# Pooling stage: tokens loaded first, band table converted on GpSimd, smaller scaling blocks, new engine orders

## What is computed

```python
def rmsnorm(x, g):
    xf = x.astype(jnp.float32)
    return xf * lax.rsqrt(jnp.mean(xf * xf, axis=-1, keepdims=True) + EPS) * g

def pool_mixer(h, w, scale):             # L = 272 tokens, D = 1024
    for g, win in enumerate((2, 4, 8, 16)):
        xg = hf[..., g * 256:(g + 1) * 256]
        cs = jnp.cumsum(xg, axis=1)
        lag = jnp.pad(cs[:, :-win], ((0, 0), (win, 0), (0, 0)))
        cnt = jnp.minimum(pos + 1, win)[None, :, None]
        outs.append((cs - lag) / cnt - xg)
    pooled = jnp.stack(outs, axis=2)
    return jnp.einsum('blgc,gcd->blgd', pooled, w).reshape(B, L, D) * scale

h = h + pool_mixer(rmsnorm(h, norm_mix), pool_w, pool_scale)
h = h + swiglu(rmsnorm(h, norm_ffn), w_gate, w_up, w_down)
```

## Time and profile before

| | |
|---|---|
| three runs | 1027.3, 1028.75, 1030.66 us |
| the profiled execution | 1028.95 us, of which the span of the engines' work is 1027.1 us and 1.85 us lie around it |
| TensorE busy | 992.3 us |
| mean granted TensorE clock over the span | 0.986 of full speed |

### The profile page before, as it was taken

How to read it: one execution, slowest core, us unless ns; L and a number is a source line. 1 busy time by engine, 2 the same in 40 slices (tenths; PEclk the granted TensorE clock), 3 DMA queues, 4 the chain that set the end, 5 groups by cost and what they waited for, 6 DMA issues and landing times.

```text
span 1027.1 us, 19786 instructions
## 1 busy us (share of the span) xinstructions
PE 992.3 (97%) x7900; PEld 963.3 (94%) x7900; DVE 816.1 (79%) x1350; ACT 521.2 (51%) x839; POOL 174.6 (17%) x178
## 2 busy tenths in 40 slices
PE   8999999999999899999999999789999999999997
PEld 6999999999988799999999998668999999999996
DVE  4887889985999889989898679999776787676542
ACT  5644443344666546464535347575445565545332
POOL 4400000220333351400056100000001330000011
PEclk7999999999999999999999999999999999999998
DMA  8467667894333348877687324342334565555541
GB/s 321 168 210 221 218 204 240 272 333 164 124 123 123 104 125 322 276 265 245 209 273 249 125 65 157 113 144 84 123 103 146 177 212 177 192 169 189 158 143 41
DMA packets 53685, 187.69 MB, mean 183 GB/s; under 512 B 6104, under 2 KB 7801, under 8 KB 53146
## 3 DMA queue, kind: packets, MB, share of 16 engines
q1 hardware_dynamic: 53594, 186.42, 54.8%
HBM read 185.35 MB, written 1.05 MB: 181 GB/s over the span
## 4 chain that ended last, share of the span: by engine, by line
PE 85%; DVE 10%; issue 2%; ACT 1%; DMA 1%; POOL 0%; SPq 0%; DVEq 0%; POOLq 0%; ACTq 0%
PE psum L429 84%; DVE memr L962 3%; DVE memr L976 2%; PE psum L444 1%; DVE memr L1015 1%; DVE mem L1148 1%; DMA mem<-in_pool_first 1%; ACT memr L1599 1%; DVE psum L1358 1%; DVE mem L1366 0%; DVE mem L1340 0%; ACT mem L1859 0%; DVE mem L1342 0%; DVE mem L1364 0%; DVE mem L1010 0%
## 5 line engine op out<-in xcount | busy, mean ns | idle before, releaser
L429 PE MATMUL psum<-memr 128*128 128x256 f32 (+5 forms) x7640 | 954.9, 288 | 24.2 <-DVE memr L976 11.7
L429 PEld LDWEIGHTS psum<-memr 128*128 128x128 f32 (+2 forms) x7640 | 932.9, 190 | 44.1 <-issue 24.4
L962 DVE TENSOR_TENSOR memr<-mem,memr 128x1024 fp32r<-128x1024 f32 (+1 forms) x290 | 357.4, 1269 | 49.8 <-ACT memr L1596 49.8
L1596 ACT ACTIVATE memr<-mem 128x1024 fp32r<-128x1024 f32 (+2 forms) x296 | 290.4, 1027 | 28.0 <-DMA mem<-in_w_down 10.4
L1599 ACT ACTIVATE memr<-mem 128x256 fp32r<-128x256 f32 (+4 forms) x168 | 80.3, 489 | 275.8 <-DVE mem L1078 113.7
L976 DVE TENSOR_TENSOR memr<-mem,memr 128x256 fp32r<-128x256 f32 (+2 forms) x129 | 63.8, 502 | 12.8 <-ACT memr L1599 12.1
L1599 ACT ACTIVATE memr<-psum 128x256 fp32r<-128x256 f32 (+4 forms) x112 | 44.8, 438 | 41.7 <-PE psum L444 23.2
L1063 DVE TENSOR_TENSOR mem<-psum,mem 128x256 f32<-128x256 f32 (+1 forms) x66 | 28.0, 424 | 47.6 <-PE psum L429 47.6
L972 DVE CUSTOM_DVE_ANT_0 mem<-mem 128x1024 f32<-128x1024 f32 x48 | 62.6, 1304 | 0.6
L2070 POOL TENSOR_TENSOR mem<-mem 128x256 f32<-128x256 f32 (+1 forms) x6 | 4.0, 671 | 314.5 <-DVE mem L1094 150.7
L976 DVE TENSOR_TENSOR memr<-psum,memr 128x256 fp32r<-128x256 f32 (+4 forms) x96 | 45.8, 496 | 12.8 <-ACT memr L1599 11.5
(11 more groups left out here) (138 smaller groups left out, 458.9 us busy)
## 6 DMA issues: line engine op xcount, KB each, us to landing
mem<-in_w_gate SPq DMA_DIRECT2D x66, 512.0 KB, 4.4
mem<-in_w_up SPq DMA_DIRECT2D x66, 512.0 KB, 4.5
mem<-in_w_ada SPq DMA_DIRECT2D x48, 512.0 KB, 4.6
mem<-in_w_down SPq DMA_DIRECT2D x48, 448.0 KB, 4.3
mem<-in_w_in SPq DMA_DIRECT2D x40, 512.0 KB, 3.7
mem<-in_w_down SPq DMA_DIRECT2D x24, 512.0 KB, 4.5
mem<-in_sb_qkv SPq DMA_DIRECT2D x24, 512.0 KB, 4.6
mem<-in_sb_o SPq DMA_DIRECT2D x8, 512.0 KB, 4.3
```

What stands on the lines that cost most here:

```text
L429: return pe.matmul(out, a, b, start=start, stop=stop)
L962: dve.tensor_tensor(r(ol, n), raw(e), rf(oh, n), ALU.subtract).then_inc(w_lo, 1)
L1596: act.activation(r(oh, n), raw(e), ACT.Copy).then_inc(w_hi, 1)
```

## The change

1. **Loads.** The token blocks are loaded in the order 0, 2, 1. The first-token table and a new small table (its low part, now computed on the host) follow, then the band table, as a tensor of its own. The constants move behind six weight tiles, epsilon becomes a memset, and `SILC` moves behind three more weight tiles, for which SyncE waits on GpSimd.
2. **Conversions.** VectorE no longer converts the two tables; GpSimd does, in two copies, before its weight tiles. Its subtraction for the low part goes. The host makes the high part exactly representable.
3. **Scaling.** The tokens are scaled in blocks of 256, 256 and 512 columns instead of 512 and 512.
4. **Waits.** The reciprocal no longer stands behind the wait for the tables, and the root no longer waits for the constants. TensorE waits for the tokens per `pooled(i)`, and for the constants in `mean_square`.
5. **Orders.** TensorE: `pool_mix(0)` and `(1)` come before `pooled(4)` and `pooled(6)`; 7 warm-up products instead of 8. VectorE and ScalarE follow. On ScalarE, weight tile 4 stands behind `pool_norm(0)` and tile 5 behind `pool_norm(1)`. The one Silu over `SILC` moves from m = 0 to m = 2 of the first SwiGLU.

```diff
-    WARM, NWARM = st.take(512), 8
+    WARM, NWARM = st.take(512), 7
+    XCOLS = ((0, 256), (256, 256), (512, 512))
...
 (TensorE)
         def pooled(i):
             g = i // 2
+            pe.wait_ge(x_lo, (3, 6, 9, 9)[g])
...
-        pe.wait_ge(pre_dve, 6)
-        pe.wait_ge(pre_pool, 2)
-        pe.wait_ge(x_lo, 3)
+        pe.wait_ge(pre_pool, 3)
         for i in range(4):
             pooled(i)
-        pe.wait_ge(x_lo, 6)
+        pool_mix(0)
         pooled(4)
         pooled(5)
-        pool_mix(0)
+        pool_mix(1)
         pooled(6)
         pooled(7)
-        pool_mix(1)
         pool_mix(2)
         pool_mix(3)
...
 (VectorE)
-        dve.wait_ge(band_in, 32)
-        dve.tensor_copy(r(BH, 4 * 144), f(BAND, 4 * 144)).then_inc(pre_dve, 1)
         dve.wait_ge(pre_act, 2)
         dve.reciprocal(f(SS + 6, 3), f(SS + 3, 3)).then_inc(pre_dve, 1)
-        dve.tensor_copy(r(BH + 4 * 144, 4 * T0, 0, 16), f(BAND + 4 * 144, 4 * T0, 0, 16)).then_inc(pre_dve, 1)
...
+        scaled_low(0)
+        scaled_low(1)
+        pooled_low(0)
+        pooled_low(1)
+        scaled_low(2)
+        pooled_low(2)
+        pooled_low(3)
         pool_add(0)
+        pooled_low(4)
+        pooled_low(5)
+        pool_norm(0)
+        pool_add(1)
         pooled_low(6)
         pooled_low(7)
-        pool_add(1)
-        pool_norm(0)
+        pool_norm(1)
         pool_add(2)
-        pool_norm(1)
+        pool_norm(2)
         pool_add(3)
-        pool_norm(2)
         pool_norm(3)
         low_halves(W_FFN[0] + 6)
...
 (ScalarE)
-        act.wait_ge(cst_in, 16)
         act.activation(f(SS + 3, 3), f(SS, 3), ACT.Sqrt, bias=epsc).then_inc(pre_act, 1)
...
+        scaled_high(0)
+        high_halves(1)
+        scaled_high(1)
         act.wait_ge(vec_in, 16)
-        for i in range(4):
-            pooled_high(i)
-        high_halves(6)
+        pooled_high(0)
+        pooled_high(1)
+        high_halves(2)
+        scaled_high(2)
+        pooled_high(2)
+        pooled_high(3)
+        high_halves(4)
         pooled_high(4)
         pooled_high(5)
         pool_norm(0)
+        high_halves(5)
         pooled_high(6)
         pooled_high(7)
-        for g in range(1, 4):
-            pool_norm(g)
+        pool_norm(1)
+        high_halves(6)
+        pool_norm(2)
+        pool_norm(3)
         high_halves(W_FFN[0] + 6)
...
 (GpSimd)
-        pool.wait_ge(pre_dve, 6)
-        pool.tensor_tensor(firsts(r, BL, 16), firsts(f, BAND + 4 * 144, T0), firsts(rf, BH + 4 * 144, T0),
-                           ALU.subtract).then_inc(pre_pool, 1)
+        pool.wait_ge(first_in, 32)
+        pool.tensor_copy(r(BH + NBAND, NALL - NBAND, 0, 16), f(BAND + NBAND, NALL - NBAND, 0, 16)).then_inc(pre_pool, 1)
+        pool.wait_ge(band_in, 16)
+        pool.tensor_copy(r(BH, NBAND), f(BAND, NBAND)).then_inc(pre_pool, 1)
...
 (SyncE)
-        for i, (lo, n) in enumerate(ROWS):
+        for i in (0, 2, 1):
+            lo, n = ROWS[i]
             sp.dma_start(f(HTOK + D * i, D, 0, n), T["htok"][lo:lo + n]).then_inc(htok_in[i], 16)
-        sp.dma_start(f(CST, C_POOL), T["cst"][:, 0:C_POOL]).then_inc(cst_in, 16)
-        sp.dma_start(f(BAND, 4 * 144), T["cst"][:, C_POOL:]).then_inc(band_in, 16)
-        sp.dma_start(f(BAND + 4 * 144, 4 * T0, 0, 16), T["pool_first"]).then_inc(band_in, 16)
+        sp.dma_start(f(BAND + NBAND, 4 * T0, 0, 16), T["pool_first"]).then_inc(first_in, 16)
+        sp.dma_start(f(BAND + NBAND + 4 * T0, 4 * 16, 0, 16), T["pool_rest"]).then_inc(first_in, 16)
+        sp.dma_start(f(BAND, NBAND), T["band"]).then_inc(band_in, 16)
+        raws(1)
         sp.dma_start(f(VEC, NVEC), T["vecs"]).then_inc(vec_in, 16)
-        raws(NRAW)
+        raws(4)
         sp.dma_start(f(H, KT * T0), T["ht"]).then_inc(h_in, 16)
+        raws(6)
+        sp.dma_start(f(CST, NCONST), T["cst"]).then_inc(cst_in, 16)
+        raws(9)
         sp.dma_start(f(SILC, 2048), T["c2"].partition_broadcast(128)).then_inc(c_in, 16)
```

More of the change, by code:

```diff
@@ L29 @@
     NVEC += _c
-C_ID, C_ONE, C_EPS, C_TRI, C_POOL = 0, 128, 256, 257, 433
-NCONST = C_POOL + 4 * 144
+C_ID, C_ONE, C_TRI, NCONST = 0, 128, 256, 432
+NBAND = 4 * 144
 ROWS = ((16, 128), (0, 16), (144, 128))
@@ L44, in constants @@
     c[:, C_ONE:C_ONE + 128] = 1.0 / D
-    c[:, C_EPS] = EPS
     q, k = np.arange(128)[:, None], np.arange(176)[None, :]
     c[:, C_TRI:C_TRI + 176] = np.where(k < q, 0.0, NEG)
-    first = np.zeros((16, 4 * T0), np.float32)
+    band, first = np.zeros((128, NBAND), np.float32), np.zeros((16, 4 * T0), np.float32)
     for g, w in enumerate(WINDOWS):
         s, t = np.arange(128)[:, None], np.arange(144)[None, :]
-        c[:, C_POOL + 144 * g:C_POOL + 144 * (g + 1)] = ((t >= s) & (t < s + w)) / w - (t == s)
+        band[:, 144 * g:144 * (g + 1)] = ((t >= s) & (t < s + w)) / w - (t == s)
         s, t = np.arange(16)[:, None], np.arange(T0)[None, :]
@@ L54, in constants @@
         first[:, T0 * g:T0 * (g + 1)] = np.where((t >= s) & (t < s + w), np.float32(1) / count, np.float32(0)) - (t == s)
-    return c, first
+    high = (first.view(np.uint32) & np.uint32(0xFFFFF000)).view(np.float32)
+    rest = np.concatenate([(first - high)[:, T0 * g:T0 * g + 16] for g in range(4)], axis=1)
+    return c, band, high, rest
 def tables():
@@ L213, in build @@
     AH, AL = top.take(KT * T0), top.take(KT * T0)
-    CST = top.take(C_POOL)
+    CST, EPSC = top.take(NCONST), top.take(1)
     VEC = top.take(NVEC)
@@ L234, in build @@
     XH, XL = st.take(3 * D), st.take(3 * D)
-    NBAND = 4 * 144 + 4 * T0
-    BAND, BH, BL = st.take(NBAND), st.take(NBAND), st.take(4 * 16)
+    NALL = NBAND + 4 * T0 + 4 * 16
+    BAND, BH = st.take(NALL), st.take(NALL)
+    BL = BH + NBAND + 4 * T0
+    XCOLS = ((0, 256), (256, 256), (512, 512))
     SS = st.take(11)
-    WARM, NWARM = st.take(512), 8
+    WARM, NWARM = st.take(512), 7
     sil = Area(WORDS - 3 * 1024, WORDS)
@@ L305, in build @@
     OUTS = ((0, 2), (2, 2), (4, 2), (6, 1), (7, 1))
-    ident, ones, epsc = f(CST + C_ID, 128), f(CST + C_ONE, 128), f(CST + C_EPS, 1)
+    ident, ones, epsc = f(CST + C_ID, 128), f(CST + C_ONE, 128), f(EPSC, 1)
     def vec(name, i=0, p1=128):
@@ L319, in a_lo @@
         return r(AL + i * T0 + n0, n)
-    def firsts(m, o, w):
-        return m(o, 4 * w, 0, 16).rearrange("p (g w) -> p g w", g=4)[:, :, 0:16]
     def pb(b, n=512, p0=0, p1=128, at=0):
@@ L457, in mean_square @@
             b = bank(("ms", root), root_done, root)
+            pe.wait_ge(cst_in, 16)
             pe.wait_ge(sq_done, 7 * (s + 1))
@@ L469, in x @@
                 return r(half + D * src + 128 * i, 128, 0, n)
-            fb = r(BH + 4 * 144 + T0 * g, T0, 0, 16)
+            fb = r(BH + NBAND + T0 * g, T0, 0, 16)
             mm(pb(b, T0), x(XH, 1, 16), fb, True, False)
@@ L976, in minus @@
             return dve.tensor_tensor(out, x, hi, ALU.subtract)
+        dve.memset(f(EPSC, 1), EPS)
         dve.memset(f(SS, 11), 1.0).then_inc(pre_dve, 1)
@@ L986, in vector, with scaled_low @@
                                      op0=ALU.mult, op1=ALU.add, accum_out=f(SS + i, 1, 0, n)).then_inc(pre_dve, 1)
-        dve.wait_ge(band_in, 32)
-        dve.tensor_copy(r(BH, 4 * 144), f(BAND, 4 * 144)).then_inc(pre_dve, 1)
         dve.wait_ge(pre_act, 2)
         dve.reciprocal(f(SS + 6, 3), f(SS + 3, 3)).then_inc(pre_dve, 1)
-        dve.tensor_copy(r(BH + 4 * 144, 4 * T0, 0, 16), f(BAND + 4 * 144, 4 * T0, 0, 16)).then_inc(pre_dve, 1)
[L992 to L997, removed]
+        def scaled_low(c):
+            for i in range(3):
+                o, w, n = D * i + XCOLS[c][0], XCOLS[c][1], ROWS[i][1]
+                dve.wait_ge(x_hi, 3 * c + i + 1)
+                dve.scalar_tensor_tensor(r(XL + o, w, 0, n), f(HTOK + o, w, 0, n), f(SS + 6 + i, 1, 0, n),
+                                         rf(XH + o, w, 0, n), ALU.mult, ALU.subtract).then_inc(x_lo, 1)
         def pooled_low(i):
@@ L1609, in scalar, with scaled_high @@
         act.wait_ge(pre_act, 1)
-        act.wait_ge(cst_in, 16)
         act.activation(f(SS + 3, 3), f(SS, 3), ACT.Sqrt, bias=epsc).then_inc(pre_act, 1)
[L1612 to L1617, removed]
+        act.wait_ge(pre_dve, 4)
+        def scaled_high(c):
+            for i in range(3):
+                o, w, n = D * i + XCOLS[c][0], XCOLS[c][1], ROWS[i][1]
+                copy(r(XH + o, w, 0, n), f(HTOK + o, w, 0, n), f(SS + 6 + i, 1, 0, n)).then_inc(x_hi, 1)
         def pooled_high(i):
@@ L1654, in ffn @@
                     act.activation(f(SROOT, n), pb(bank_of["ms", root], n), ACT.Sqrt, bias=epsc).then_inc(root_done, 1)
-                    if i == 0:
-                        act.wait_ge(c_in, 16)
-                        act.activation(f(SILC, 2048), f(SILC, 2048), ACT.Silu).then_inc(silc_done, 1)
+                if i == 0 and m == 2:
+                    act.wait_ge(c_in, 16)
+                    act.activation(f(SILC, 2048), f(SILC, 2048), ACT.Silu).then_inc(silc_done, 1)
                 act.wait_ge(gate_ev, c)
```

(2 more changed lines are left out.)

6 lines of the change are left out of this document (2 added, 4 removed).

## The result

The changed kernel takes 1035.62 us (median of eight runs, 1033.55 to 1038.56) against 1029.10 (eight runs, 1027.23 to 1031.46): a ratio of 1.0066, 95% interval 1.0047 to 1.0085, or 6.5 us slower. The forecast of 1026.3 with its range up to 1030.0 missed it, and on the wrong side. The ratios leave out one slow execution, of experiment 10, with 1250.44 us at a mean granted clock of 0.721.

The account below looks back on a forecast made before the run. TensorE, busy 992.3 of 1027.1 us, was taken as the bound, its early waits and low clock as the openings. 1.1 us from the orders plus 3.4 x 0.43 from the clock gave 2.6 us: 1026.3, range 1023.0 to 1030.0.

Parts of the forecast that it names:

- The reciprocal leaves the table's wait: Front: the reciprocal follows the root, so token scaling starts at about 9.0 instead of 10.11, 1.1 us sooner.
- Smaller blocks: Front: with 256-column blocks, first scaled copy to last low half takes 1.9 us instead of 2.84.
- GpSimd converts: Front: table copies take 1.8 and 0.9 us, plus 0.6 for contention; `pooled(0)` starts at 11.6 instead of 13.09.
- Idle gap: TensorE between warm-up and `pooled(0)`: one product fewer, gap 1.7 us instead of 2.37.
- Case C: Early TensorE: the clock never falls, or only for an instant, thanks to the shorter gap; 1023.0 us, chance 0.13.
- Orders, tile 5: First SwiGLU: tile 5's low half ends at 33.7, TensorE loses 0.7; `gate_up(0,1)` starts at 39.4, 1.1 us sooner.
- The step to 18.4: Early TensorE: `pooled` 0 to 3 run from 11.6, the first at 1.0 us, then 1.8 each, ending at 18.4.
- GpSimd's squares: Ahead of `mean_square`: 14 instructions from 33.7 end at 44.5 to 46.0, TensorE wants them at 45.45; counted 0.
- F: GpSimd bounds both ends: slow copies, tile 5 and squares late; no gain up to 1.5 us slower, 1030.5; chance 0.08.
- Moved loads and Silu: Constants, `SILC` and Silu at m = 2: all in time, counted 0; 1.5 us if the Silu's cover were gone.
- The clock: Early TensorE: when full clock returns decides the rest, 0.43 us per us; likeliest at about 23, 2.6 us gained, chance 0.30.
- E: Early TensorE: split mixes bring the clock back late, at 31 to 33; 0.7 us slower, 1029.6; chance 0.13.

Follow-up runs that it names:

- experiment 10: experiment 3 repeated on another chip: 1026.44 us, ratio to the kernel before 0.9973.
- experiment 9: experiment 3 with eight warm-up products, 1026.32 us; then also one wide matmul ahead of each `pooled`, 1026.12, or two, 1025.63.
- experiment 6: Changed kernel with GpSimd's six additions of the first norm's squares on one column instead of 272: 1030.20 us, ratio to the kernel before 1.0006.
- experiment 3: Changed kernel with ScalarE copying weight tiles 4 and 5 early again, right behind tiles 2 and 3: 1026.79 us, ratio to the kernel before 0.9977.
- experiment 8: experiment 3 with the Silu over `SILC` back at m = 0: 1029.65 us, ratio to the kernel before 0.9990.
- experiment 5: Changed kernel with only its front kept (loads, conversions, blocks, waits), orders of before, tiles 4 and 5 early: 1028.17 us, ratio to before 0.9988.
- experiment 4: Kernel before with only ScalarE's copies of tiles 4 and 5 moved behind `pool_norm(0)` and `pool_norm(1)`: 1037.68 us, ratio to before 1.0074.
- experiments 1 and 2: `mean_square` one weight pair later, behind `gate_up(0,2)`: on the changed kernel 1027.76 us; on the kernel before, as control, 1030.11 us.

## Why the prediction was wrong, step by step

- **The reciprocal leaves the table's wait: right, and worth more than I took.** Block 1's square starts at 6.52, the root at 7.77, scaling at 8.31 (forecast 9.0; before 10.11).
- **Smaller blocks: right, 0.2 short.** Three copies of 256 columns took 1.30, as taken; from the first copy to the last low half were 2.1 us, not 1.9.
- **GpSimd converts: right, within its bounds.** Timeline after:

```profile
7.21 1.52 POOL L2103 CAST memr<-mem 16x1152 fp32r<-16x1152 f32 x1 [5.96 <-DMA mem<-in_pool_rest]
8.69 0.66 POOL L2105 CAST memr<-mem 128x576 fp32r<-128x576 f32 x1
```

  I took 1.8 and 0.9. They were done at 9.4, a microsecond ahead of the last low half, so my 0.6 for two streams at once was not needed; the first low halves took 1.56. `pooled(0)` began at 10.56, released by VectorE, instead of 11.6: 2.5 us earlier than before. The sum was on the safe side by a microsecond.
- **Idle gap: wrong mechanism.** Case C's "for it" was the shorter gap. The gap was 0.37 us and the clock fell at 13.4 all the same. In experiment 9 it fell during `pooled` work with no gap ahead of it, and stayed up with two wide matmuls ahead of each. With one trace of each, that points to what TensorE does in the stage and not to the gap.
- **Orders, tile 5: the time right, partly by luck.** Its low half ended at 33.48 (forecast 33.7). But the wait of 0.7 did not come: TensorE, slowed, began `gate_up(0,0)` only at 34.0 (forecast 32.6). And in after's chain the tile follows a norm that the low clock had delayed; with a return at 20.1 (experiment 6) TensorE waited 1.35 for it. The step to 18.4 has a slip of 0.4: 11.6, 1.0 and three times 1.8 make 18.0.
- **GpSimd's squares: this step failed.** The start was right, 33.44 against 33.7. The term was 14 instructions of 0.63 to 0.9, ending at 44.5 to 46.0 ("Cover just suffices"), counted as 0 with bounds 0 and 0.6. TensorE's wait for them was 4.73. Measured: five at 0.77 to 0.85, eight at 1.61 to 1.64, one at 0.63, ending at 51.4. All that I priced from the earlier trace rows ran while VectorE did 272-column work, but for the end of the last one; I moved the instructions behind 37 us, beside 1024-column tiles, and kept their price. A clue stood in my own rows: the first tile of L962 took 1.59 beside GpSimd's last square. Those behind it took 1.21 (the row above). I had even charged such an excess to the front (3.21 against 2.08) and not here. Even by that mild ratio, 1.31, five instructions of 0.85 and then nine of 1.1 would have ended at 33.7 + 4.2 + 10.0 = 47.9, and TensorE would have waited some 2.5 us from 45.45. `mean_square` would then have begun at 47.9, against 46.68 before: a slowdown, on the forecast's own figures. I also gave the step no case of its own: F held its price to 1.5 us in all.
- **Moved loads and Silu: 0 holds** in the traces (experiments 3 and 8); the Silu's median is inconclusive.
- **The clock: E came in the profile (33.9), but not for E's reason.** Its mechanism was that split mixes bring it back late. The returns, all in us: with split mixes 33.9, 32.6, 20.2, 19.6, 20.1, 21.3 and 33.8; with unsplit ones 26.4 and 25.5 (before, its control), 23.8 (experiment 5) and 34.7 (experiment 4). Both orders give earlier and later returns, so the split alone doesn't decide it. Experiments 3 and 8, with the same order on TensorE, gave 20.2 and 33.8; what decides stays open. It is worth up to 4.0 us in one execution.
- **The rest of the sum: the size came out, in part by luck.** With the two copies early again, the change gives 1026.79 and 1026.44 against medians of 1029.0 and 1029.9 before: 2.2 and 3.5 less, where I forecast 2.6. But experiment 3's trace gets there on another path: the clock is back at 20.2 and not 23, the mark lies at 36.09, 4.4 ahead, VectorE's norms are on the chain from 22.65 on, where I had taken VectorE off it, and 1.7 are lost near the attention mixer. The change as made pays 8.8 us in the medians for two moved copies. The traces show 6.6 of them, at an equal clock; the rest goes with a mean granted clock of 0.982 against 0.987 (medians), and why that differs stays open.
- **That the change does what it says is no argument** that its waits stay away: every wait that it removes was the last in the chain, and a new one, of a part I had off the chain, came behind them.

## What to carry to other kernels

When a step moves in time, price it anew from what runs beside it in its new place, not from its old rows: here two-input work of 272 columns on GpSimd cost about double beside VectorE's long two-input instructions, and slowed VectorE too. Before a copy on ScalarE is moved back, follow its whole line of heirs, here copy, low half, 14 instructions of squares, `mean_square`; where the slack behind is under a microsecond, that is a case with a chance and a price, and an idle TensorE may pay again in clock. An independent stretch of TensorE's work (`gate_up(0,2)`) ahead of the consumer buys cover back, and costs nothing where none is missing (experiments 1 and 2).

## What the runs showed of the hardware

- One column of an addition on GpSimd takes 0.19 us alone and 1.05 beside VectorE's two-input tiles of 1024 columns, and 272 columns of a square 0.64 and 1.63: almost the same excess per instruction, 0.86 and 0.99.
- It goes the other way too: two low halves of 272 columns on VectorE took 0.91 us with GpSimd idle (after, 23.28) and 3.18 beside GpSimd's two-input subtraction of 1024 columns (experiment 3, 23.15).
- TensorE's clock fell from 2.4 to 1.2 GHz during unbroken `pooled` work, and returned after some 7 us at the low level in experiment 3 (13.4 to 20.2) and some 20 in experiment 8 (13.3 to 33.8), with the same order on TensorE. In the one execution profiled with two wide matmuls ahead of each `pooled` it stayed at 2.4 GHz through the whole stage.
- GpSimd's copy to the reduced type took 1.52 us for 1152 columns and 0.66 for 576, 1.3 (16 rows) and 1.15 ns (128 rows) a column; its two-input subtraction took 2.36 for 1024, 2.3 ns a column.
